# Second mixer: the norm stage taken out, the norm's weight and hi/lo split straight from the residual, the token factor put on the products

## The reference

```python
for l in range(2):
    x = x + 0.5 * swiglu(rmsnorm(x, ffn1_norm[l]), ...)
    h = rmsnorm(x, mix_norm[l])            # x * rsqrt(mean(x*x) + 1e-6) * weight
    parts = split(h @ w_in[l], split_at)   # the projection of the mixer
    o = concatenate(mla(parts), nsa(parts), stick_breaking(parts))
    x = x + o @ w_out[l]
    x = x + 0.5 * swiglu(rmsnorm(x, ffn2_norm[l]), ...)
```

## Time and profile before

| | us |
|---|---|
| three runs | 3958.51, 3973.25, 3974.38 |
| median | 3973.25 |
| time of the profiled execution | 3963.0 |
| its span | 3961.1 |
| PE busy | 3397.4 (86% of the span) |
| DVE busy | 1731.5 (44%) |
| ACT busy | 1035.2 (26%) |
| POOL busy | 268.6 (7%) |
| granted TensorE clock, mean | 0.927 of full speed |

### The profile page before, as it was taken

How to read it: one execution, slowest core, us unless ns; L and a number is a source line. 1 busy time by engine, 2 the same in 40 slices (tenths; PEclk the granted TensorE clock), 3 DMA queues, 4 the chain that set the end, 5 groups by cost and what they waited for, 6 DMA issues and landing times. The chain is left out here.

```text
span 3961.1 us, 39195 instructions
## 1 busy us (share of the span) xinstructions
PE 3397.4 (86%) x15298; PEld 2414.1 (61%) x15298; DVE 1731.5 (44%) x2473; ACT 1035.2 (26%) x1475; POOL 268.6 (7%) x230
## 2 busy tenths in 40 slices
PE   4988986768787778699978889999899798889997
PEld 3465665333463223588856457888788675557886
DVE  2747757464533000444234654442443235645433
ACT  2121221120321000422132453221322223443222
POOL 1110010020111000000001100000000102000001
PEclk6999998889888999799989899999999999899998
DMA  1101000101101993222121012221322121013221
...
DMA packets 49390, 326.24 MB, mean 82 GB/s; under 512 B 6896, under 2 KB 7280, under 8 KB 11120
## 3 DMA queue, kind: packets, MB, share of 16 engines
...
...
## 5 line engine op out<-in xcount | busy, mean ns | idle before, releaser
L358 PE MATMUL psum<-ffn_x_hi,ffn_w_hi 128*128 128x512 f32 x1408 | 551.4, 392 | 13.8 <-DVE ffn_x_lo L314 13.8
L358 PE MATMUL psum<-ffn_x_lo,ffn_w_hi 128*128 128x512 f32 x1408 | 550.9, 391 | 0.0
L358 PE MATMUL psum<-ffn_x_hi,ffn_w_lo 128*128 128x512 f32 x1408 | 550.5, 391 | 0.0
L303 DVE TENSOR_TENSOR ffn_w_lo<-ffn_raw,ffn_w_hi 128x2048 fp32r<-128x2048 f32 x128 | 293.4, 2292 | 420.8 <-ACT ffn_w_hi L274 420.8
L104 PE MATMUL psum<-mix_normed,mix_ring 128*128 128x512 f32 x832 | 373.9, 611 | 64.8 <-DMA mix_ring<-w_ssd 32.0
L274 ACT ACTIVATE ffn_w_hi<-ffn_raw 128x2048 fp32r<-128x2048 f32 x128 | 245.2, 1916 | 573.0 <-PE psum L358 573.0
L104 PEld LDWEIGHTS psum<-mix_normed,mix_ring 128*128 128x128 f32 x832 | 162.6, 197 | 273.3 <-issue 230.5
L358 PEld LDWEIGHTS psum<-ffn_x_hi,ffn_w_hi 128*128 128x128 f32 x1408 | 266.4, 189 | 75.2 <-DVE ffn_w_lo L310 20.0
L358 PEld LDWEIGHTS psum<-ffn_x_hi,ffn_w_lo 128*128 128x128 f32 x1408 | 266.1, 189 | 55.8
L358 PEld LDWEIGHTS psum<-ffn_x_lo,ffn_w_hi 128*128 128x128 f32 x1408 | 266.2, 189 | 55.6
L358 PE MATMUL psum<-ffn_hid_hi,ffn_w_hi 128*128 (+1 forms) x704 | 273.9, 389 | 0.0
...
## 6 DMA issues: line engine op xcount, KB each, us to landing
ffn_raw<-w_ffn SPq DMA_DIRECT2D x128, 1024.0 KB, 4.8
mix_ring<-w_experts SPq DMA_DIRECT2D x48, 1024.0 KB, 13.7
mix_ring<-w_mix SPq DMA_DIRECT2D x36, 1024.0 KB, 4.9
mix_normed<-w_experts SPq DMA_DIRECT2D x24, 1024.0 KB, 14.7
experts_work<-w_experts SPq DMA_DIRECT2D x24, 1024.0 KB, 15.7
mix_ring<-w_gdn SPq DMA_DIRECT2D x16, 1024.0 KB, 4.8
mix_ring<-w_ssd SPq DMA_DIRECT2D x10, 1024.0 KB, 6.9
mix_ring<-w_out SPq DMA_DIRECT2D x8, 1024.0 KB, 6.5
```

What stands on the lines that cost most here:

```text
L303: dve.tensor_tensor(w_lo[:, q, :], raw[:, q, :], w_hi[:, q, :].bitcast(F32), ALU.subtract)\
L358: ins = pe.matmul(out, wp[:, q, w], xp, start=start and a == 0, stop=stop and a == 2)
```

## The change

`mixer2` no longer calls `resid_norm_stage`. `project2` gets the weight column and does the norm's work itself:

- `hi` and `lo` of x are made from `resid` and the weight (ScalarE copy with the weight as scale; VectorE multiply and subtract in one instruction).
- PE computes the sum of squares in two forms at the start of the stage: repeated over the partitions (bank 7), and with tokens on the partitions (bank 6, four matmuls with one column). Both become factors: `rstd` (128 x 512) and `by_token` (128 x 4).
- Output tiles are multiplied by `rstd` as they leave PSUM, all 15 of them on VectorE (`take`); values and gates by `by_token`.
- Slab 0 comes in four pieces of 128 x 512, and PE works on tiles 0 and 1 together, k-tile by k-tile, as the pieces are split. The ring has four slots, so slabs 1 to 3 are issued at once behind the pieces.
- The square roots stand on ScalarE behind the four pieces, the reciprocals on VectorE behind them and before slab 1's `lo` part.

```diff
-def project2(nc, m, b, slabs):
+def project2(nc, m, b, slabs, gain):
...
-    x = m.ring[:, 2:4, :].rearrange("p s n -> p (s n)").rearrange("p (k t) -> p k t", k=KD)
+    rstd, by_token = cut(m.norm_tmp, 0, T), cut(m.norm_tmp, T, NT)
+    pieces = 4
+    piece = lambda j: slice(j * (SLAB // pieces), (j + 1) * (SLAB // pieces))
...
-        gate_in = m.ring[:, gate_slab % 2, :].rearrange("p (k n) -> p k n", k=KD)[:, :, P:P + GATES]
+        raw = lambda i: m.ring[:, i % SLOTS, :]
+        gate_in = raw(gate_slab).rearrange("p (k n) -> p k n", k=KD)[:, :, P:P + GATES]
...
-            landed = sem(2)
-            x_hi_done, x_done, hi_done, split, projected, read_v, read_a, gate_split = sem(8)
+            landed, piece_in = sem(SLOTS), sem(pieces)
+            x_hi_done, x_done, hi_done, split, projected, read, gate_split, gates_in = sem(8)
+            summed, mean, rooted, inverted = sem(4)
...
-                for i in range(n_slabs):
-                    if i >= 2:
-                        sp.wait_ge(split, i - 1)
-                    sp.dma_start(m.ring[:, i % 2, :], slabs[i]).then_inc(landed[i % 2], 16)
+                for j in range(pieces):
+                    sp.dma_start(raw(0)[:, piece(j)], slabs[0][:, piece(j)]).then_inc(piece_in[j], 16)
+                for i in range(1, n_slabs):
+                    if i >= SLOTS:
+                        sp.wait_ge(split, i - SLOTS + pieces)
+                    sp.dma_start(raw(i), slabs[i]).then_inc(landed[i % SLOTS], 16)
...
-                for n in range(TILES2):
+                pe.matmul(m.ps[:, 7, :], m.ones, m.squares, start=True, stop=True).then_inc(summed, 1)
+                for t in range(NT):
+                    ins = pe.matmul(m.ps[:, 6, t:t + 1], m.squares[:, tok(t)], m.ones[:, 0:1], start=True, stop=True)
+                ins.then_inc(summed, 1)
+                for k in range(KD):
+                    pe.wait_ge(split, k // 2 + 1)
+                    pe.wait_ge(x_done, k + 1)
+                    for n in range(2):
+                        ins = three_parts(pe, m.ps[:, n, :], ws(0, k, n * P), xs(k), k == 0, k == KD - 1)
+                        if k == KD - 1:
+                            ins.then_inc(projected, 1)
+                for n in range(2, TILES2):
                     i, at = n // 2, n % 2 * P
-                    pe.wait_ge(split, i + 1)
+                    pe.wait_ge(split, i + pieces)
                     if n >= 4:
-                        pe.wait_ge(read_a if n % 2 else read_v, (n - 4) // 2 + 1)
+                        pe.wait_ge(read, n - 3)
                     for k in range(KD):
-                        if n == 0:
-                            pe.wait_ge(x_done, k + 1)
                         ins = three_parts(pe, m.ps[:, n % 4, :], ws(i, k, at), xs(k), k == 0, k == KD - 1)
                     ins.then_inc(projected, 1)
                 pe.wait_ge(gate_split, 1)
+                pe.wait_ge(inverted, 2)
                 for i in (8, 9):
-                    pe.wait_ge(split, i + 1)
+                    pe.wait_ge(split, i + pieces)
                     for t in range(NT):
                         if i == 8:
-                            pe.wait_ge(read_a if t in (0, 2) else read_v, (6, 7, 7, 8)[t])
+                            pe.wait_ge(read, TILES2 - 3 + t)
                         for k in range(4):
                             g = 4 * (i - 8) + k
                             three_parts(pe, gate_bank(t), xs(g, tok(t)), (gate_hi[:, g, :], gate_lo[:, g, :]),
...
-                    act.wait_ge(landed[i % 2], 16 * (i // 2 + 1))
+                    act.wait_ge(landed[i % SLOTS], 16 * (i // SLOTS + (i % SLOTS > 0)))
...
-                    act.activation(w_hi[:, i % 2, :], m.ring[:, i % 2, :], ACT.Copy).then_inc(hi_done, 1)
-
-                hi_part(0)
-                for k in range(KD):
-                    act.activation(x_hi[:, k, :], x[:, k, :], ACT.Copy).then_inc(x_hi_done, 1)
-                hi_part(1)
-                for i in range(n_slabs - 2):
-                    n = 2 * i + 1
-                    if n < TILES2:
-                        act.wait_ge(projected, n + 1)
-                        act.activation(b.f[:, n, :], m.ps[:, n % 4, :], ACT.Copy, scale=tile_scale(n)).then_inc(read_a, 1)
-                    hi_part(i + 2)
+                    act.activation(w_hi[:, i % 2, :], raw(i), ACT.Copy).then_inc(hi_done, 1)
+
+                for j in range(pieces):
+                    act.wait_ge(piece_in[j], 16)
+                    act.activation(w_hi[:, 0, piece(j)], raw(0)[:, piece(j)], ACT.Copy).then_inc(hi_done, 1)
+                    for k in (2 * j, 2 * j + 1):
+                        act.activation(x_hi[:, k, :], m.resid[:, k, :], ACT.Copy, scale=gain[:, k:k + 1])\
+                            .then_inc(x_hi_done, 1)
+                act.wait_ge(mean, 2)
+                act.activation(rstd, rstd, ACT.Sqrt).then_inc(rooted, 1)
+                act.activation(by_token, by_token, ACT.Sqrt).then_inc(rooted, 1)
+                for i in range(1, n_slabs):
+                    hi_part(i)
                 for t in (1, 3):
                     act.wait_ge(projected, TILES2 + 1 + t)
-                    act.activation(b.v[:, t, :], m.ps[:, 4 + t, :], ACT.Copy)
-                act.wait_ge(read_v, 10)
+                    act.activation(b.v[:, t, :], m.ps[:, 4 + t, :], ACT.Copy, scale=by_token[:, t:t + 1])
+                act.wait_ge(gates_in, NT)
                 act.activation(b.gates, b.gates, ACT.Sigmoid)
...
-                    dve.wait_ge(hi_done, i + 1)
+                    dve.wait_ge(hi_done, i + pieces)
...
-                    dve.tensor_tensor(w_lo[:, i % 2, :], m.ring[:, i % 2, :], w_hi[:, i % 2, :].bitcast(F32),
+                    dve.tensor_tensor(w_lo[:, i % 2, :], raw(i), w_hi[:, i % 2, :].bitcast(F32),
...
-                lo_part(0)
-                for k in range(KD):
-                    dve.wait_ge(x_hi_done, k + 1)
-                    dve.tensor_tensor(x_lo[:, k, :], x[:, k, :], x_hi[:, k, :].bitcast(F32), ALU.subtract)\
-                        .then_inc(x_done, 1)
+                def take(n):
+                    dve.wait_ge(projected, n + 1)
+                    dve.scalar_tensor_tensor(b.f[:, n, :], m.ps[:, n % 4, :], tile_scale(n), rstd, ALU.mult, ALU.mult)\
+                        .then_inc(read, 1)
+
+                def gate(t):
+                    dve.scalar_tensor_tensor(b.gates[:, t, :], gate_bank(t), by_token[:, t:t + 1], m.gate_bias,
+                                             ALU.mult, ALU.add).then_inc(gates_in, 1)
+
+                dve.wait_ge(summed, 2)
+                dve.tensor_scalar(rstd, m.ps[:, 7, :], 1.0 / D, EPS, ALU.mult, ALU.add).then_inc(mean, 1)
+                dve.tensor_scalar(by_token, m.ps[:, 6, 0:NT], 1.0 / D, EPS, ALU.mult, ALU.add).then_inc(mean, 1)
+                for j in range(pieces):
+                    dve.wait_ge(hi_done, j + 1)
+                    dve.tensor_tensor(w_lo[:, 0, piece(j)], raw(0)[:, piece(j)], w_hi[:, 0, piece(j)].bitcast(F32),
+                                      ALU.subtract).then_inc(split, 1)
+                    for k in (2 * j, 2 * j + 1):
+                        dve.wait_ge(x_hi_done, k + 1)
+                        dve.scalar_tensor_tensor(x_lo[:, k, :], m.resid[:, k, :], gain[:, k:k + 1],
+                                                 x_hi[:, k, :].bitcast(F32), ALU.mult, ALU.subtract)\
+                            .then_inc(x_done, 1)
+                dve.wait_ge(rooted, 2)
+                dve.reciprocal(rstd, rstd).then_inc(inverted, 1)
+                dve.reciprocal(by_token, by_token).then_inc(inverted, 1)
                 lo_part(1)
-                for i in range(n_slabs - 2):
-                    n = 2 * i
-                    dve.wait_ge(projected, n + 1)
-                    dve.tensor_scalar(b.f[:, n, :], m.ps[:, n % 4, :], tile_scale(n), None, ALU.mult)\
-                        .then_inc(read_v, 1)
-                    lo_part(i + 2)
-                for t in (0, 2):
+                dve.wait_ge(inverted, 2)
+                for i in range(2, n_slabs):
+                    for n in (2 * i - 4, 2 * i - 3):
+                        if n < TILES2:
+                            take(n)
+                    lo_part(i)
+                for t in range(NT):
                     dve.wait_ge(projected, TILES2 + 1 + t)
-                    dve.tensor_copy(b.v[:, t, :], m.ps[:, 4 + t, :])
-                    if t == 0:
-                        dve.tensor_tensor(b.gates[:, 0, :], gate_bank(0), m.gate_bias, ALU.add).then_inc(read_v, 1)
-                dve.wait_ge(projected, TILES2 + NT)
-                dve.tensor_tensor(b.gates[:, 1:, :], m.ps[:, 0:3, 0:GATES],
-                                  m.gate_bias.unsqueeze(1).to_broadcast([P, NT - 1, GATES]), ALU.add)\
-                    .then_inc(read_v, 1)
+                    gate(t)
+                    if t % 2 == 0:
```

(5 more changed lines are left out.)

## The result

| | before | changed |
|---|---|---|
| median, us | 3971.37 (5 runs) | 3934.72 (5 runs) |
| lowest and highest | 3958.51, 3974.38 | 3927.98, 3940.85 |
| span of the profiled execution | 3961.1 | 3936.1 |
| PE busy | 3397.4 | 3410.7 |
| PEclk, mean | 0.927 | 0.930 |

The ratio is 0.9917, with a 95% interval of 0.99 to 0.9933: 36.65 us by the medians, between 27 and 40 by the interval. The changed kernel was run again in two other series beside the kernel before, with medians of 3935.28 (6 runs, before 3969.51) and 3934.46 (6 runs, before 3968.90): 34.2 and 34.4 us.

What follows compares the result with a forecast made beforehand. PE, busy 86% of the span, was the bound, with only the hole ahead of the projection to gain. 36.9 less 0.2 gave 36.7 us: 3926.3 from the profiled execution, 3936.6 from the median; forecast 3930, range 3916 to 3948.

Steps and rivals of the forecast that it cites:

- The hole: Norm stage ahead of the projection: PE busy only 1.10 of 24.60 us; tile 2 forecast 18.6 and 18.25 us earlier.
- the 36.7 of the sum: Whole kernel: 36.9 us gained up to tile 2 in two layers, less 0.2 us at the stage ends.
- Start of PE: PE's first projection product at P+5.5 and P+6.1 us, P being the start of PE's first instruction of the norm stage.
- the earliest bound of tile 2: Projection: tile 2 starts at P+17.8 us at the earliest, if ScalarE never waits for a piece.
- rival (b): Slab 0's pieces land late, sharing DMA engines with slabs 1 to 3; gain 12 us smaller, 3938 us; chance 4%.
- Slab 1: Projection: slab 1's `lo` part ready at P+18.7 us, so PE waits 0.2 to 0.4 us before tile 2.
- What was costed at nothing: Rest of the projection: VectorE's 15 reads, 3.8 us per slab beside PE's 10.8, later `hi` parts and GpSimd cost nothing.
- The tail term: End of the projection: ScalarE's last scaled copy of values costs at most 0.1 us more per layer, 0.2 in all.
- (a): Projection, tiles 0 and 1: all 48 matmuls run at the low clock; gain 20.3 us, time 3943; chance 4%.
- (c): Projection: VectorE as only reader makes PE wait for banks once a read costs 4.3 us; slower than before; chance 2%.
- (d): Projection: norm only moved, root, table load and reciprocal (5.3 us) ahead of slab 1; 3936 if 5 us later; chance 4%.

Runs made afterwards that it cites:

- reads of 4.0 us: The changed kernel with one more VectorE reciprocal ahead of each read of an output tile; 3930.00 us, ratio 0.991 to the kernel before.
- reads of 4.9 us: The changed kernel with one more VectorE reciprocal and two multiplies by 1 ahead of each output tile read; 3977.11 us, ratio 1.0023 to the kernel before.

## Why the prediction was right

**The hole.** The forecast took the time from the start of the norm stage to tile 2, and that is where the gain is. At tile 2 it is 19.90 + 18.19 = 38.1 us; 36.9 were forecast, with bounds of 35.3 and 38.7. Up to the heads 37.8 are left of it, against the 36.7 of the sum. Without the pieces it is 28.1.

**Start of PE.** Forecast P+5.5 and P+6.1, bounds P+4.9 and P+6.4; measured P+4.79 and P+5.75. The eight one-column passes took 1.66 and 1.71 us (2.0 assumed), and the first VectorE row came when they were done, at P+2.63. In layer 0 the sum and the passes ended at P+2.59 where 3.1 was added up (they overlap by 0.17 us, and the passes were 0.34 shorter), and the two means took 0.67 us together where 0.89 was allowed. From piece 0 on VectorE to PE's first product it is 1.49 us (1.51 forecast). These small terms all erred to one side, and P+4.79 lies 0.1 us below the bound. ScalarE began piece 0 at P+2.62, before VectorE was free for it.

**The pieces.** The estimate let piece 1 come at P+5.43, as in `ffn1`. It was there by P+4.38 and ScalarE never waited again, which is the case from which the earliest bound of tile 2 (P+17.8) was made; tile 2 of layer 0 came 0.4 us before even that, PE and slab 1's `lo` part both being early. The later pieces do land later (2.5 us after the issue for the first, a median of 3.8 for the four), and slab 1 after 7.5 in place of 4.8: they are slower together, as rival (b) says, but each landing after the first is ahead of its turn on ScalarE, which waits for none of them.

**Slab 1.** Forecast: PE waits 0.2 to 0.4 us and tile 2 starts at P+18.7 in both layers. Measured: a wait of 0.22 us and P+17.42 in layer 0, none and P+18.76 in layer 1. In layer 0 PE and the `lo` part were both some 1.2 us early and still met within 0.2 us: that the wait itself came out as forecast is luck. In layer 1 the `lo` part ended at P+18.1, and PE's own 13.0 us from P+5.75 decide; the forecast had 12.4 from P+6.1, two errors that all but cancel, with ten matmuls at the low clock for seven. Table load 1.28, root 0.63, reciprocal 3.35, slab 2.26 are the rows of before. On the table load the prediction weighed a rule of the Trainium skill ("ScalarE: Activation LUTs", "What ACT_TABLE_LOAD costs"), by which 1.38 us of drain follow it. The trace does not agree: in its new place too the root starts 0.02 us after the load's end (2004.18 + 1.28 to 2005.48). The row decides, and here the load costs 1.28.

**What was costed at nothing.** The 15 reads on VectorE: 0.691 us each, with 36.3 us of waiting for PE among them. Their cover is deep: reads of 4.0 us are still hidden but for 1.3 us in each layer, at slab 8, and reads of 4.9 us cost 32.9 in the two. The four-slot ring, the gates and GpSimd's lost multiplies show nowhere. The tail term of 0.2 us is what it was, 0.18 from PE's last product to the heads over both layers: ScalarE's copies of values 0.69 us for 0.60, the gates' writes 0.24 for 0.21, and the table load behind them 1.28 again.

**The rivals.** (a) The clock: in layer 0 seven or eight matmuls ran low, in layer 1 ten or, in one execution, 13, and at most 14 with any edit; each more costs 0.2 us, and there is no gap between k-tiles. (b) discussed above, no cost. (c) The threshold is real and not reached with reads of 0.69 us. Its account was too simple, though: beyond it PE waits for slab parts (`project_w_lo`), not for banks, and the single tile of slab 7 makes slab 8 the first and longest wait. By the rival's own sum reads of 4.9 us would cost 1.3 us at each of 14 slabs, 18 in all, and they cost 32.9. (d) is true as a statement and free because of its place: put ahead of the pieces the same work costs 8.9 us.

**The absolute number.** The sum gave 3926.3 from the profiled execution and 3936.6 from the median of the runs shown; the second is 1.9 us from the measured median, the first 8.4. I had leaned to the first. That step was the weakest: the profiled execution of before was not typical. Over the executions of before, those under 3960 us have a mean granted clock of 0.928 to 0.930 and those above 3972 one of 0.924 to 0.926, so the clock goes with the time; that it is the recurrences' clock is seen only in profiles of the changed kernels (642.4 to 652.7 us), since before has one profile. Luck has a part in the total too: 36.7 forecast and 36.65 measured agree better than they should, since the two later series gave 34.2 and 34.4, and the 3.5 us that the heads of layer 1 take back were in no term of the sum. The level is to be taken from the median, and the gain of a stage from the stage; the gain of the program can be some us less.
